# Replacing the gathered experts of the last two prompt tiles by a dense pass over all experts

## The reference, cut to what matters

```python
def _peer(h, wq, subkeys, u, v):            # h: RMS-normed tokens (512 prompt, 32 sample), D = 1024
    q = (t @ wq).reshape(blk, 8, 128)       # 8 heads
    s1 = einsum('thd,hnd->thn', q[..., :64], subkeys[:, 0])   # 128 keys each
    s2 = einsum('thd,hnd->thn', q[..., 64:], subkeys[:, 1])
    v1, i1 = top_k(s1, 16); v2, i2 = top_k(s2, 16)
    sc, pos = top_k(v1[..., None] + v2[..., None, :], 16)     # 16 of 256 pairs
    e = i1[pos // 16] * 128 + i2[pos % 16]                    # expert number
    g = softmax(sc)
    a = gelu(einsum('td,thkd->thk', t, u[e]))
    return einsum('thk,thkd->td', g * a, v[e])                # 128 (head, k) slots a token
```

## Time and profile before

| | us |
|---|---|
| median of three runs | 1834.46 |
| span of the profiled execution | 1831.0 |
| TensorE busy | 1256.7 |
| VectorE busy | 1307.8 |
| ScalarE busy | 580.0 |
| bytes moved by DMA | 696.47 MB, of them 570.53 MB by gathers |

### The profile page before, as it was taken

One profiled execution on the slowest core, in us unless ns is written; L12 is line 12 of the kernel. 1 busy time (PEld: TensorE's weight loads), 2 busy tenths in 40 slices (PEclk: granted clock), 3 DMA queues, 4 the chain that ended last, 5 costly groups with the idle time before them and its releaser, 6 DMA issues.

```text
span 1831.0 us, 26290 instructions
## 1 busy us (share of the span) xinstructions
PE 1256.7 (69%) x8990; PEld 693.1 (38%) x8990; DVE 1307.8 (71%) x3842; ACT 580.0 (32%) x2009; POOL 522.6 (29%) x569
## 2 busy tenths in 40 slices
PE   8989746678778565788877485889878543434353
PEld 3666612344444222455445132556536111111111
DVE  5561495888766577898767667898757768686754
ACT  2331223424323233334422333334423222222222
POOL 0100032333322323332323322322323333333332
PEclk9999859778798778788898587887997555555555
DMA  6325499999999999999999999998999999999997
GB/s 263 94 99 174 149 426 408 403 425 425 421 424 421 422 421 401 396 425 398 424 423 421 425 382 404 424 413 330 421 423 419 425 427 426 426 426 426 426 422 306
DMA packets 119380, 696.47 MB, mean 380 GB/s; under 512 B 17983, under 2 KB 21118, under 8 KB 49102
## 3 DMA queue, kind: packets, MB, share of 16 engines
q0 software_dynamic: 78848, 570.53, 74.7%
q1 hardware_dynamic: 36686, 121.83, 17.6%
q10 hardware_dynamic: 3712, 2.43, 0.4%
HBM read 691.65 MB, written 3.02 MB: 379 GB/s over the span
## 4 chain that ended last, share of the span: by engine, by line
DMA 37%; PE 27%; DVE 22%; issue 5%; ACT 4%; POOL 1%; ACTq 0%; DVEq 0%; POOLq 0%
DMA rows<-in_peer_uv,index 28%; DVE rows L2349 9%; PE ps_v L1600 6%; PE ps_f L1420 4%; PE ps_f L1470 3%; PE ps_f L1449 3%; DMA wch<-in_w_row 3%; PE ps_f L1214 3%; DMA wch<-in_w_out 2%; PE ps_h L1580 2%; DMA wch<-in_peer_wq 2%; PE ps_f L1435 1%; DVE score L2074 1%; DMA wch<-in_w_ukv 1%; PE ps_f L1298 1%
## 5 line engine op out<-in xcount | busy, mean ns | idle before, releaser
L1191 POOL DMA_INDIRECT rows<-in_peer_uv,index x544 | 512.7, 943 | 1211.4 <-PE ps_v L1600 1010.4
L2349 DVE CUSTOM_DVE_ANT_0 rows<-rows,ps_h 128x1024 f32<-128x1024 f32 x544 | 657.5, 1220 | 271.7 <-DMA rows<-in_peer_uv,index 228.7
L1600 PE MATMUL ps_v<-rows,diag 128*32 128x256 f32 x4352 | 434.2, 515 | 462.4 <-ACT diag L1910 462.1
L1600 PEld LDWEIGHTS ps_v<-rows,diag 128*32 128x32 f32 x4352 | 125.9, 133 | 719.2 <-ACT diag L1910 612.2
L1901 ACT ACTIVATE tan<-arg 128x2 f32<-128x2 f32 x272 | 55.4, 204 | 784.4 <-DVE arg L2359 765.4
L1904 ACT ACTIVATE weight<-tan,lead 128x1 f32<-128x1 f32 x544 | 180.8, 379 | 9.1
L1910 ACT ACTIVATE diag<-sel,weight 128x32 f32<-128x32 f32 x544 | 140.7, 305 | 0.0
L1420 PEld LDWEIGHTS ps_f<-bufh,wch 128*128 128x128 f32 x768 | 114.4, 233 | 22.0 <-issue 19.6
L1420 PE MATMUL ps_f<-bufh,wch 128*128 128x128 f32 x768 | 121.3, 323 | 0.0
L1214 PE MATMUL ps_f<-wch,bufh 128*128 128x512 f32 (+1 forms) x192 | 80.4, 559 | 18.3 <-DMA wch<-in_w_row 18.0
L1449 PE MATMUL ps_f<-wch,bufb 128*128 128x512 f32 x96 | 53.1, 693 | 18.4 <-DMA wch<-in_w_out 18.4
(11 more groups left out here) (359 smaller groups left out, 1675.8 us busy)
## 6 DMA issues: line engine op xcount, KB each, us to landing
wch<-in_w_gate SPq DMA_DIRECT2D x60, 512.0 KB, 8.1
wch<-in_w_row SPq DMA_DIRECT2D x36, 512.0 KB, 11.3
wch<-in_w_o SPq DMA_DIRECT2D x32, 512.0 KB, 7.8
wch<-in_w_out SPq DMA_DIRECT2D x32, 512.0 KB, 10.1
wch<-in_peer_wq SPq DMA_DIRECT2D x32, 512.0 KB, 10.6
rows<-in_peer_uv,index POOLq DMA_INDIRECT x544, 13.8
w_tok<-in_w_tok SPq DMA_DIRECT2D x4, 1640.0 KB, 13.7
wch<-in_w_uq SPq DMA_DIRECT2D x6, 384.0 KB, 4.9
```

The lines of the kernel that those rows point to most:

```text
L1191: pool.indirect_dma_start(rows[c % RING][:, :, :].rearrange("p a d -> p (a d)"), None, io.peer_uv[:, :], at).then_inc(s_uv[c % RING], 16)
L1600: ins = nc.tensor.matmul(ps_v[GROUP * a:GROUP * (a + 1), :], diag[:, c % DRING, :], rows[c % RING][:, 1, QD * a:QD * (a + 1)], start=False ...
L2349: v.tensor_tensor_reduce(out=u, in0=u, in1=ps_h[:, :], scale=1.0, scalar=0.0, op0=ALU.mult, op1=ALU.add, accum_out=dots[:, c % KEEP:c % KE ...
```

## The change

Tiles 3 and 4 (the last two prompt tiles, `DENSE = (3, 4)`) no longer gather. For their 256 tokens *all* 16384 experts are computed, and the weights of those that a token didn't choose are zero.

- Only blocks 0 to 8 have columns: `NCOL` is 9 x 32 = 288. `RING` is 8.
- The three fronts' 351 ticks now go evenly through columns 0 to 223 (`FRONT_COLS`, `ticks_at`); front(1) ends in column 74, front(2) in 149, front(3) in 223.
- The choosing has a table of its own (`choices`): blocks 1 to 4 in columns 2 to 45, one part a column; 5 to 8 in columns 75 to 118; 9 to 12 in columns 150 to 173, two parts a column; 13 to 16 in columns 224 to 239, three parts a column. `index` and `half_w` have six buffers. For dense tiles, `choose` transposes both key numbers and the weight into `slot_i`, `slot_j`, `slot_w` (128 slots x 256 tokens).
- From column 241 (`DENSE_COL`) each column carries one tick of a generator `dense`, and the rest of it follows the columns. It has an opening tick, 32 *builds*, and 66 ticks of *pairs*; 32 more builds stand ahead of the pair tick 34.
- A build makes the weights of 8 tokens for all 128 second keys j and 64 first keys i: VectorE compares rows of numbers with the slots (`hots`), TensorE multiplies the one-hot matrices (`build`, eight products 128x128 with 64 columns), ScalarE copies the result out of PSUM in two pieces (`keep`) to `g_low` and `g_high`.
- A pair handles two groups of 128 experts (those with one first key). `load_u` and `load_v` on SyncE's queue bring 512 KB each, three buffers for either. `inner`: eight products with 256 columns a group into one bank. `take` (ScalarE) copies it, `cubed`, `gated_in`, `finish` (VectorE) and `bend` (ScalarE tanh) make gelu times weight. `outer`, two ticks later: four products with 512 columns a group, accumulated in four banks over 32 pairs. `gather_sums` (VectorE) adds the banks to x after each half; the end stores x.
- For tile 3 the normed columns go to `hrows[1]`, for tile 4 to `both`; x has three buffers (`XB`), and `load_x` waits for an earlier residual.
- `peer_ut`, u in a transposed layout, is a new input; the semaphores of the dense pass are those of the first stage, used on (`Carried`).

```diff
-NCOL = NB * SG
-RING = 9
+DENSE = (3, 4)
+NG = sum(i not in DENSE for i, _ in BLOCKS)
+NCOL = NG * SG
+RING = 8
...
+FRONT_COLS = 224
+DENSE_COL = 241
+TW = len(DENSE) * P
+HALVES = 2
+NI = NKEY // HALVES
+NLOW = 18
+HOT = 4
+BUILDS = TW // (2 * HOT)
+PAIRS = NKEY // 2
+EDGE = PAIRS // HALVES
+NSTREAM = 3
...
 def ticks_at(b):
 
-    p = b // SLOTS + 1
-    if p >= NP:
-        return 0
-    n, k = Ticks(p).all + Ticks(p).base, b % SLOTS
-    done = lambda k: n * min(k, SLOTS - 4) // (SLOTS - 4)
-    return done(k + 1) - done(k)
+    done = lambda k: ticks_through(NP - 1) * min(k, FRONT_COLS) // FRONT_COLS
+    return done(b + 1) - done(b)
...
             def load_x(i):
                 t = tile(i)
-                if i >= 2:
-                    sp.wait_ge(s_xc, first_block(i - 1))
+                if i >= 3:
+                    sp.wait_ge(s_xc, first_block(i - 2))
...
+            def load_u(e):
+                if e >= NSTREAM:
+                    sp.wait_ge(s_ux.sem, s_ux.upto(e - NSTREAM + 1))
+                sp.dma_start(u_in[e % NSTREAM][:, :], io.peer_ut[e, :, :]).then_inc(s_u[e % NSTREAM].sem, 16)
...
+            for e in range(NSTREAM, NKEY + 4):
+                if e < NKEY:
+                    load_u(e)
+                if e - 4 >= NSTREAM:
+                    load_v(e - 4)
...
+            def build(n):
+                half = n // BUILDS
+                if half and n % BUILDS == 0:
+                    pe.wait_ge(s_sum.sem, s_sum.upto(4 * half))
+                if n >= 4:
+                    pe.wait_ge(s_kept, n - 3)
+                for b in range(2):
+                    r = 2 * n + b
+                    pe.wait_ge(s_hot, r + 1)
+                    for q in range(HOT):
+                        at = NI * (HOT * b + q)
+                        ins = nc.tensor.matmul(ps_f[:, n % 4, at:at + NI], hot_j[:, r % 2, q, :], hot_i[:, r % 2, q, :],
+                                               start=True, stop=True)
+                    ins.then_inc(s_built, 1)
+
+            def inner(n):
+                if n == 0:
+                    pe.wait_ge(s_both, 1)
+                else:
+                    pe.wait_ge(s_act.sem, s_act.upto(n))
+                for a in range(2):
+                    e = 2 * n + a
+                    pe.wait_ge(s_u[e % NSTREAM].sem, s_u[e % NSTREAM].upto(16 * (e // NSTREAM + 1)))
+                    w = u_in[e % NSTREAM][:, :].rearrange("p (c k) -> p c k", c=DC)
+                    for k in range(DC):
+                        ins = nc.tensor.matmul(ps_f[:, 4, TW * a:TW * (a + 1)], w[:, k, :], both[:, k, :],
+                                               start=(k == 0), stop=(k == DC - 1))
+                    ins.then_inc(s_ux.sem, 1)
+
+            def outer(n):
+                pe.wait_ge(s_made.sem, s_made.upto(n + 1))
...
+                    first, final = n % EDGE == 0 and a == 0, n % EDGE == EDGE - 1 and a == 1
+                    for t in range(len(DENSE)):
+                        for c in range(2):
+                            ins = nc.tensor.matmul(ps_f[:, 2 * t + c, :], act_x[:, n % 3, a, P * t:P * (t + 1)],
+                                                   v_in[e % NSTREAM][:, 512 * c:512 * (c + 1)], start=first, stop=final)
+                    ins.then_inc(s_vx.sem, 1)
...
+            def hots(n):
...
+                for b in range(2):
+                    r, at = 2 * n + b, t + HOT * b
+                    if r >= 2:
+                        dve.wait_ge(s_built, r - 1)
+                    v.tensor_tensor(hot_j[:, r % 2, :, :], last(slot_j[:, at:at + HOT], NKEY), mid(row_i[:, :], HOT),
+                                    ALU.is_equal)
+                    for q in range(HOT):
+                        ins = v.tensor_scalar(hot_i[:, r % 2, q, :], row_i[:, NI * half:NI * (half + 1)],
+                                              slot_i[:, at + q:at + q + 1], slot_w[:, at + q:at + q + 1],
+                                              ALU.is_equal, ALU.mult)
+                    ins.then_inc(s_hot, 1)
+
+            def cubed(n):
+                x, e = act_x[:, n % 3, :, :], act_e[:, n % 2, :, :]
+                dve.wait_ge(s_act.sem, s_act.upto(n + 1))
+                if n >= 2:
+                    dve.wait_ge(s_made.sem, s_made.upto(n - 1))
+                step(v.scalar_tensor_tensor(out=e, in0=x, scalar=CUBE, in1=x, op0=ALU.mult, op1=ALU.mult), s_step)
+                v.scalar_tensor_tensor(out=e, in0=e, scalar=1.0, in1=x, op0=ALU.add, op1=ALU.mult).then_inc(s_cubed.sem, 1)
```

313 lines of the change are left out of this document (270 added, 43 removed).

## The result

The changed kernel takes 2507.09 us, the median of four runs (2501.98 to 2508.09), against 1835.58 (1833.58 to 1840.53) for the kernel before on the same chip: 1.364 times as long, interval 1.361 to 1.367. Forecast were 2425 us, range 2330 to 2570. The direction and the mechanism came as forecast; the centre was 82 us too low. The profiled execution has a span of 2506.2 us.

The account below looks back on a forecast made before the run. DMA bounds the old kernel; after the change TensorE's float32 dense pass decides. Terms 238.1 + 950 + 88 + 129 + 912 + 10 + 88 + 6 = 2421 us of span, plus 3.5 outside: 2425 us, range 2330 to 2570.

Parts of the forecast that it names:

- The bound: Dense pass: TensorE's float32 products set the time, 14.25 us a pair of expert groups, 912 us for 64 pairs.
- sustained price: Rival in the dense pass: 512-column bf16 matmuls at 131 ns, dense pass 556 us, total 2065 us; chance 1%.
- The cover of the loads: Dense pass: 512 KB loads land in 11.3 us, every slot has 13.8 us, one pair, so they are hidden.
- Columns 0 to 223: Three fronts packed under fewer columns; VectorE or TensorE largest in seven of twelve windows; 950 us, bounds 880 and 1050.
- Columns 224 to 240: Last tile's four blocks are chosen here: 84 us of VectorE against 42 us of gathers; 88 us, DMA waits.
- The builds: Gate weights: first builds under columns 241 to 273 take 129 us, second 32 builds amid the pairs 88 us.
- Hidden unless the clock is low: TensorE's part of a first build: 2.0 us at the high level, about 3.4 at the low one, otherwise hidden.
- DMA as the bound from first to last: Rival for the whole kernel: transfers set the time, some 1490 us, 19% faster; chance 1%.
- the interlock: Rival in the fronts: closer ticks stall the engines to 0.75, 860 becomes 1147 us, total 2620; chance 6%.
- The rival of a low clock in the builds: TensorE's clock falls in the builds, costing 60 us more, inside the forecast range; chance 4%.
- a dent of some 85 us with VectorE at 9: Sign in the changed profile: in the middle of the dense pass, about 85 us with VectorE at 9.

Follow-up runs that it names:

- the run over 256 columns: Changed kernel with the three fronts spread over 256 columns instead of 224 and the dense pass starting at column 273 instead of 241: 2536.65 us.
- the run with wider streams: Changed kernel with six of eight one-hot products in each build streaming 128 columns instead of 64, same result: 2467.62 us, ratio to before 1.345.
- VectorE's two instructions: Changed kernel with four tensor_scalars in each half build replaced by two tensor_tensors: 2503.48 us alone; together with the wider build products 2456.11 us.

## Why the prediction held, and what was mis-sized

**The bound.** Right. The dense pass is TensorE's float32 arithmetic: TensorE is busy throughout, half the inner products take away their own time, half as many loads again cost nothing, and 16 bits turn it into transfers. The pair was read off the fronts' records as 14.25 us and measured 13.77, so that 912 became 881; what stands beside the pairs came to 19 us instead of 10. (The sum for `inner` has a slip: 16 x 0.22 is 3.5, and its 3.6 is 16 x the 0.227 of the line; it is worth 0.2 us a pair.) The Trainium skill ("TensorE: Matmul & The Clock Gate", section "Back-to-back issue gap") gives for an isolated product that streams N columns at the high level a spacing of N / 2.4 + 2.5 ns. Twice that, as the prediction took a float32 record, would be an estimated 0.432 us for 512 columns and 0.218 for 256; the trace agrees, with 0.429 and 0.216. The sustained price of 131 ns, which the Trainium skill sets beside it there, shows nowhere in the 900 us of the pairs. Nor does it show where the dense products are in 16 bits: four records of 512 columns, each with its own weights, take 0.90 us from start to start, 0.225 each:

```profile
1967.04 1.06 PE L1789 MATMUL ps_f<-vin,actx 128*128 128x512 bf16 x4
1967.94 1.07 PE L1789 MATMUL ps_f<-wch,actx 128*128 128x512 bf16 x4
```

**The cover of the loads.** Right, and larger than reckoned: with three buffers a `load` has a pair's time, 13.8 us, and lands in 4 to 5.

**Columns 0 to 223**, forecast 950, measured 976. The step was the sum over windows of the largest engine's work, divided by how far an engine fills its window; I took 0.90 for the windows that VectorE or TensorE bound. Three of the twelve in the trace, cut as the sum cut them:

```profile
473.30:553.60 80.30, 64.89 (x444) 42.49 (x436) 35.53 (x91) 22.40 (x64) 14.98 (x16) 0.93 0.95 378
...
640.60:727.90 87.30, 64.58 (x376) 38.66 (x376) 76.54 (x235) 22.64 (x78) 18.26 (x19) 0.76 0.77 283
...
882.90:997.40 114.50, 60.47 (x447) 29.58 (x445) 95.12 (x314) 31.35 (x87) 21.39 (x22) 0.76 0.82 311
```

The last is the one with two chosen parts a column. VectorE's work is what was reckoned (92 forecast, 95.12 measured), but it fills 95.12 / 114.5 = 0.83 of the window, and in the one from 640.6 it fills 0.88. In the first the transfers do (0.95). The sum over all twelve tells where the time went. In the seven windows in which the forecast had VectorE or TensorE as the largest, their work was 494 us in the forecast and 496 in the trace, but they took 570 us, a filling of 0.87 instead of 0.90: 21 us. The five in which it had the transfers took 406 us instead of 376: 30 us. Together that is 51 us above the reckoned 925, of which the 25 that were added for hand-overs covered half. So the loads were right and the filling was taken too favourably, in the windows of the transfers most. That VectorE's choosing sets the time where it is doubled is shown: without it columns 150 to 174 are 41 us shorter. That the price lies more in the windows' largest load than in the density of the ticks is what the run over 256 columns says. Which hand-overs take up the gap between the sum of 860 and the real 976 is not shown. TensorE waits most in this stage with the mixes, for their diagonals from ScalarE (us in all, times, longest),

```profile
PE ps_v L1744 <- ACT diag L2124: 152.8, 37, 16.7
```

and the 16-bit fronts leave TensorE's own work at most a part of the gap.

**Columns 224 to 240**, forecast 88, measured 108. Right in its mechanism (VectorE is busy 93 of 108 us, and DMA waits), too small by 2.2 us for each of the four blocks chosen and by the start of block 7, 11.3 us, which had no term of its own.

**The builds**, forecast 129 and 88, measured 155.7 and 119.8, 59 us more together. This is the step that failed. "Hidden unless the clock is low" was the sentence, the low clock was priced at 60 us and given 4%, and it happened. Two prices were behind it. VectorE's was too low: the timeline of the second builds (start, length, shapes, count, idle before) shows four tensor_scalars in 0.98 us,

```profile
2009.77 0.69 DVE L2639 TENSOR_TENSOR hotj<-slotj,row 128x512 f32<-128x512 f32 x1
2010.38 0.98 DVE L2642 TENSOR_SCALAR hoti<-row,sloti,slotw 128x64 f32<-128x64 f32 x4
2011.77 0.69 DVE L2639 TENSOR_TENSOR hotj<-slotj,row 128x512 f32<-128x512 f32 x1 [0.41 <-PE ps_f L1759]
```

0.245 us each, over the forecast's upper bound of 0.19; a build is 3.0 us where VectorE bounds it (the run with wider streams), instead of 2.4 to 2.6. And the last bracket shows it waiting for TensorE all the same, since TensorE at clock 0.50 needs 0.24 us a record (49 of L1759 in 11.55 us), 3.7 us a build against the 3.4 that the forecast gave for this case:

```profile
2008.67 11.55 PE L1759 MATMUL ps_f<-hoti,hotj 128*128 128x64 f32 x49
```

Of the 119.8 - 88 = 32 us in the middle, 118.1 - 96.6 = 21.5 went with the clock alone and another 6.6 with VectorE's two instructions; a build then costs 2.81 us, near the 2.6 forecast. The reason that I gave for a high clock in the pairs, that TensorE has no gaps, held there and doesn't hold as a rule: in the second builds it is in work 116.26 of 118.1 us and yet granted 0.50. The Trainium skill (the same page, section "Why this matters for your kernels") ties a fall of the clock to idle gaps between bursts of products. For the fall itself the trace agrees: it came right after 4.16 us without a product (0.91 from 1953 to 1956 us, 0.50 from there on),

```profile
1954.71 5.52 PE L1759 MATMUL ps_f<-hoti,hotj 128*128 128x64 f32 x25 [4.16 <-DVE hoti L2642]
```

but no gap accounts for the clock staying down through the 118.1 us behind it, and here the measurement decides. With the wider streams the same gap of 4.16 us stands ahead of the second builds, and the clock falls too, but it is back within some microseconds (length, busy us, clock as above):

```profile
1941.00:1945.00 4.00, 3.94 (x20) 3.78 (x19) 3.17 (x10) 0.65 (x2) 0.00 (x0) 0.50 0.00 0
1945.00:1950.00 5.00, 3.54 (x26) 3.19 (x26) 4.82 (x16) 1.19 (x4) 0.00 (x0) 0.95 0.00 0
```

That the width of the streams decides here is shown; why it does is not.

**The rivals.** DMA as the bound from first to last, the sustained price and the interlock didn't come (860 / 976 is 0.88, where it needed 0.75). Behind the first stood the right condition, the price of a group of experts, and the run with 16-bit dense products shows it on its other side. The rival of a low clock in the builds did come, with 59 us for the 60 it was priced at, at a chance of 4%; but wider streams gave back only 41 of the 59 (21.5 and 155.7 - 136 = 19.7), the rest is VectorE's price, so the match is in part luck.

**The total.** Every stage but the pairs and the end was taken too low, 108 us in all, and these two gave back 23. Little cancelled, then: the centre was low by 82 us, and the range covered it. Among the signs named beforehand, that of a dent of some 85 us with VectorE at 9 was wrong for the same reason: it is 120 us long, and TensorE fills it.

## What to carry to other kernels

Before trading gathers for a dense pass, set the transfers saved against the columns that TensorE must stream in the kernel's own type: here 256 gathered columns at 2.5 us, 640 us, against 128 groups of experts at 6.9 us of float32 products, 881 us, and the kernel lost although it moved 134 MB less. Work packed under fewer columns pays in every stretch for that stretch's largest load, so one engine's extra task costs most of its length where it was free before (here the choosing of eight blocks: 94 us for some 137 us of VectorE). Where an engine's share is "hidden at the high clock", price it at the low one too, and where its streams are short, try wider ones and look at the granted clock.

## What the runs showed of the hardware

- The granted clock can stay at 0.50 while TensorE is in work 98% of the time: products of 64 columns, each with its own 128x128 weights. The same builds with six of eight records at 128 columns were granted 0.97, and TensorE streamed 1.75 times the columns in 72 instead of 116 us. So the narrow form was the dearer one here, which I hadn't expected of any product.
- Less work for TensorE can go with a lower clock: with 16-bit products in the fronts it was 0.64 instead of 0.83 over the same 959 us of the run (one run of each kernel, on two chips; the kernel before had 0.77 and 0.76 there).
- The upper halves of float32 words can be streamed in place as 16-bit floats, with every second half word skipped, at one record a product: 16 records of 256 columns took 1.82 us from start to start where float32 takes 32 records and 6.9 us.
- Four tensor_scalars of 128x64 with two per-partition scalars take 0.98 us, more than two tensor_tensors of 128x256, which do the same work in 0.42 us each, 0.88 from the start of the first to the end of the second.
